# Second mixer's output product: another order of its weight slabs, and two of its pieces in other places among the memory units

## The chip, the cores and the metric

The kernel runs on one core of one Trainium2 chip. The metric is the time of one execution on the device in microseconds. It works on 512 tokens of 1024 features in float32; every large matrix product is made of three products of split numbers (high x high, high x low, low x high), so that a weight slab has to be split in two before TensorE can use it.

## What is computed

The reference chains two blocks of two layers each. The change lies in the second layer of the first block, in the product by `w_out[1]`:

```python
def lru_mixer(h, w_in, conv_w, conv_b, wa, ba, wx, bx, lam):
    p = h @ w_in
    xb, gate, mq = jnp.split(p, [LRU_WIDTH, 2 * LRU_WIDTH], axis=-1)
    xc = centred_depthwise_conv(xb, conv_w, conv_b)
    y = (rg_lru(xc, wa[0], ba[0], wx[0], bx[0], lam[0], False)
         + rg_lru(xc, wa[1], ba[1], wx[1], bx[1], lam[1], True))
    y = y * jax.nn.gelu(gate)
    return y, mq.reshape(B, S, MEM_HEADS, MEM_HEAD_DIM)
...
        mo = memory_attention(mq, mk, mv)
        x = x + jnp.concatenate([mixed, mo], axis=-1) @ w_out[l]
        x = x + squared_relu_mlp(rms_norm(x, mlp_norm[l]), w_up[l], w_down[l])
```

`mixed` has 1024 features (the recurrent part), `mo` 512 (the attention to the memory, 4 heads of 128), so the product has 1536 rows of weights and 1024 outputs.

## The kernel before

Everything is kept transposed: a tile is 128 features by 512 tokens. The program is written engine by engine, with the order of every engine's instructions by hand and semaphores between them; nothing is scheduled by a tool. Each engine goes through its list in order, and an instruction that waits holds up all that stands behind it on that engine.

**Weights.** They come in slabs of 128 x 2048 (16 tiles of 128 x 128). A slab passes through four hands: SP's queue loads it into `w_raw` (line 617), ScalarE rounds it to `w_hi` (`split_high`, line 1260), VectorE takes the rest to `w_lo` (`split_low`, line 1601), TensorE uses both. Each of the three buffers holds two slabs, slab s in place s mod 2. `lo_done` counts the slabs split; `mm_done` counts what TensorE has finished, four to a slab. ScalarE may split slab s when TensorE has finished slab s - 2, and the load of a slab waits until the one two before it has been split.

**The output product of the second mixer** (`out1_1`) has 6 slabs, MIX_O to MIX_O + 5. The 8 output tiles are two halves of 4 blocks, and half h, block b is summed in PSUM bank 4h + b. The 12 tiles of rows are 3 parts of 4: parts 0 and 1 are the recurrent output (`mixL`), part 2 is the memory's (`mixM`). A slab holds one part of one half. The inner function `out(h, part, b)` (matmuls on line 1091) makes one piece: 4 row tiles x 3 split products = 12 matmuls of 128x128 by 128x512. Slab number before: 3h + part. The rest of the text writes a piece as (h, part, b).

**The memory units.** The attention to the memory is 8 units M1[0] to M1[7], of one block of 128 tokens and two heads each. For a unit TensorE does `scores` (L921), `turn_probs` (transposes, L932), `weigh` (L942) and `turn_out` (transposes, L954). Between them VectorE scales and takes maxima (`front`), ScalarE does the exponentials and copies the transposed probabilities (`take_turned`, L1370), VectorE divides (`back`, L1820) and splits the output into `mixM_hi`, `mixM_lo` (`finish`, L1849 and L1851). The units use banks 4 (scores), 5 (turned probabilities) and 6 (outputs). Bank 7 holds a gate of the recurrence until `gate_read` reaches 8.

**TensorE's order before**: (0,0,0..3); the scores of two units; then the 8 units, with (0,1,0), (0,1,1) and (0,1,2) before the weigh of M1[1], M1[2], M1[3]; (0,1,3) behind the last weigh; the last `turn_out`; a wait for its split; (0,2,0..3); then half 1: (1,0), (1,1), (1,2), four blocks each; then the next phase, `up1_1_0` (L843).

**ScalarE and VectorE around it**: slab MIX_O + 2 is split before the units, MIX_O + 3 behind them. Then come the four blocks of half 0: VectorE adds each finished bank to `x` (`add`, L2028, when `mm_done` shows the block of the memory part done), ScalarE writes the scaled `xg_hi` of it (`next_high`, L1462), VectorE `xg_lo` (`next_low`, L2033), and GpSimd sums squares (L648, L652, L654). Behind these four blocks both split slabs MIX_O + 4, MIX_O + 5 and the first of the next phase, then do the four blocks of half 1 in the same way.

## Time and profile before

| | us |
|---|---|
| median of 3 runs without a profile | 3509.99 |
| lowest and highest of them | 3508.42, 3515.12 |
| the profiled execution | 3516.55 |
| its span | 3514.7 |
| TensorE busy in the span | 3331.3 (95%) |
| VectorE busy | 1794.6 (51%) |
| ScalarE busy | 1129.0 (32%) |
| GpSimd busy | 417.9 (12%) |
| mean granted clock of TensorE | 0.957 |

The profile is of one execution of its own, a little longer than the median. Times inside it count from the span's start. A matmul of 128x512 is shown with a length of 0.39 us while the next starts 0.227 us after it, because matmuls overlap in the array; what a row of them costs is read from their starts. The number in brackets at a row's end is how long the engine had been idle before it, and which instruction released it. The granted clock is 1.00 (2.4 GHz) or 0.50 (1.2 GHz), and means lie between.

### The profile page before, as it was taken

How to read it: one execution, taken by the hardware profiler on the slowest of the kernel's cores; microseconds unless marked ns; L12 is line 12 of the kernel's file. 1: busy time of each engine (PE TensorE's matmuls, PEld its weight loads, DVE VectorE, ACT ScalarE, POOL GpSimd, SP SyncE). 2: the span in 40 equal slices, each digit the busy share in tenths (PEclk: the TensorE clock that was granted, in tenths of full speed). 3: DMA queues.
4: the chain of work that ended last, by engine and by line, in shares of the span. 5: the costliest groups of instructions: out<-in, count | busy, mean ns of one | idle time of the engine just before them, and what ended most of it. 6: DMA issues, size and time to landing. Idle time of an engine off the chain costs nothing.

```text
span 3514.7 us, 40951 instructions
## 1 busy us (share of the span) xinstructions
PE 3331.3 (95%) x15310; PEld 2741.9 (78%) x15310; DVE 1794.6 (51%) x1923; ACT 1129.0 (32%) x1292; POOL 417.9 (12%) x391
## 2 busy tenths in 40 slices
PE   7999999999999999999977899999999996699998
PEld 5787888876788878888866688888888885678887
DVE  7764535378552545445355554445434436644444
ACT  3443222267321223223233233223323215223222
POOL 1001000100100060001023410002000202620002
PEclk9999999999999999999986799999999997599999
DMA  3111222322122224222310022224232320012222
GB/s 140 65 51 66 105 99 96 108 96 72 60 96 96 96 96 115 93 106 85 108 60 1 1 96 93 101 82 136 90 108 78 114 96 12 1 55 98 98 92 76
DMA packets 46189, 293.08 MB, mean 83 GB/s; under 512 B 5424, under 2 KB 5936, under 8 KB 17936
## 3 DMA queue, kind: packets, MB, share of 16 engines
q1 hardware_dynamic: 44640, 287.04, 23.2%
q0 software_dynamic: 1456, 4.79, 0.8%
q8 instruction: 61, 1.00, 0.1%
q14 instruction: 32, 0.26, 0.0%
HBM read 289.70 MB, written 2.10 MB: 83 GB/s over the span
## 4 chain that ended last, share of the span: by engine, by line
PE 87%; DVE 6%; POOL 3%; ACT 2%; issue 1%; DVEq 0%; ACTq 0%; POOLq 0%
PE ps L843 72%; POOL dec L754 3%; PE ps L942 2%; PE ps L1027 2%; PE ps L1091 2%; PE ps L1058 1%; PE ps L921 1%; PE ps L1172 1%; PE ps L932 1%; PE ps L890 1%; PE ps L901 1%; DVE mx L1791 0%; DVE w_lo L1601 0%; PE ps L873 0%; ACT sc_n L1359 0%
## 5 line engine op out<-in xcount | busy, mean ns | idle before, releaser
L843 PE MATMUL ps<-xg_hi,w_hi 128*128 128x512 f32 x2304 | 899.8, 391 | 0.0
L843 PE MATMUL ps<-xg_hi,w_lo 128*128 128x512 f32 x2304 | 896.4, 389 | 0.0
L843 PE MATMUL ps<-xg_lo,w_hi 128*128 128x512 f32 x2304 | 896.4, 389 | 0.0
L1601 DVE TENSOR_TENSOR w_lo<-w_raw,w_hi 128x2048 fp32r<-128x2048 f32 (+1 forms) x288 | 671.3, 2331 | 278.0 <-ACT w_hi L1260 278.0
L1260 ACT ACTIVATE w_hi<-w_raw 128x2048 fp32r<-128x2048 f32 (+1 forms) x288 | 545.2, 1893 | 657.5 <-PE ps L843 564.4
L843 PEld LDWEIGHTS ps<-xg_hi,w_hi 128*128 128x128 f32 x2304 | 432.7, 188 | 92.1 <-issue 2.2
L843 PEld LDWEIGHTS ps<-xg_lo,w_hi 128*128 128x128 f32 x2304 | 432.6, 188 | 91.4 <-issue 2.1
L843 PEld LDWEIGHTS ps<-xg_hi,w_lo 128*128 128x128 f32 x2304 | 432.6, 188 | 89.6
L843 PE MATMUL ps<-hid_hi,w_hi 128*128 128x512 f32 x1216 | 473.4, 389 | 0.0
L843 PE MATMUL ps<-hid_hi,w_lo 128*128 128x512 f32 x1216 | 473.0, 389 | 0.0
L843 PE MATMUL ps<-hid_lo,w_hi 128*128 128x512 f32 x1216 | 473.0, 389 | 0.0
L1702 DVE SCALAR_TENSOR_TENSOR x<-ps,x 128x512 f32 (+1 forms) x120 | 83.0, 692 | 403.0 <-PE ps L843 399.8
L1689 DVE TENSOR_TENSOR tmp<-ps,r_bc 128x512 f32<-128x512 f32 x176 | 121.6, 691 | 322.9 <-PE ps L843 307.7
L843 PEld LDWEIGHTS ps<-hid_hi,w_hi 128*128 128x128 f32 x1216 | 228.3, 188 | 48.6 <-issue 1.4
L843 PEld LDWEIGHTS ps<-hid_hi,w_lo 128*128 128x128 f32 x1216 | 228.3, 188 | 47.5
L843 PEld LDWEIGHTS ps<-hid_lo,w_hi 128*128 128x128 f32 x1216 | 228.3, 188 | 46.9
L648 POOL TENSOR_TENSOR ssq<-x 128x512 f32<-128x512 f32 x9 | 9.3, 1038 | 2046.5 <-DVE x L1702 1849.0
L1303 ACT ACTIVATE hid_hi<-tmp 128x512 f32 x88 | 55.7, 632 | 387.6 <-DVE tmp L1692 387.6
L1313 ACT ACTIVATE xg_hi<-x,vec x64 | 46.3, 724 | 350.2 <-DVE x L1702 350.2
L1301 ACT ACTIVATE tmp<-tmp 128x512 f32<-128x512 f32 x88 | 55.6, 632 | 268.9 <-DVE tmp L1689 268.9
L1166 PE MATMUL ps<-fac 64*128 64x128 f32 (+1 forms) x576 | 83.9, 412 | 39.0 <-DVE fac L2120 37.2
L1296 ACT ACTIVATE hid_hi<-tmp 128x512 f32 x64 | 39.6, 633 | 252.9 <-DVE tmp L1676 252.9
(329 smaller groups left out, 3814.6 us busy)
## 6 DMA issues: line engine op xcount, KB each, us to landing
w_raw<-up_dram SPq DMA_DIRECT2D x120, 1024.0 KB, 4.7
w_raw<-in_dram SPq DMA_DIRECT2D x42, 1024.0 KB, 4.8
w_raw<-down_dram SPq DMA_DIRECT2D x32, 1024.0 KB, 4.7
w_raw<-down_dram SPq DMA_DIRECT2D x32, 768.0 KB, 4.2
w_raw<-down_dram SPq DMA_DIRECT2D x32, 640.0 KB, 3.8
w_raw<-out_dram SPq DMA_DIRECT2D x14, 1024.0 KB, 4.7
w_raw<-out_dram SPq DMA_DIRECT2D x8, 768.0 KB, 4.2
w_raw<-memk_dram SPq DMA_DIRECT2D x4, 1024.0 KB, 4.7
```

The lines of the kernel that those rows point to most:

```text
L754: last = pool.tensor_tensor(to[:, :, u, :], (half, mid)[1 - u], (mid, half)[1 - u], ALU.subtract)
L843: last = pe.matmul(ps[:, 2 * q + b, :], (w_hi, w_lo)[wp][:, q, t:t + P], parts[xp], start=(k == 0 and m == 0), stop=(k == p.ktiles - 1 and ...
L942: last = pe.matmul(ps[:, u.o_bank, u.o_col + i * u.d:u.o_col + (i + 1) * u.d], turned(u)[:, kb, i * P:(i + 1) * P], u.v[kb][i], start=(kb ...
L1027: last = pe.matmul(ps[:, bank + b, :], (w_hi, w_lo)[wp][:, j % 2, t:t + P], (xg_hi, xg_lo)[xp][:, k, :], start=(k == 0 and m == 0), stop=( ...
L1091: last = pe.matmul(ps[:, 4 * h + b, :], (w_hi, w_lo)[wp][:, s % 2, t:t + P], parts[xp], start=(part == 0 and k == 0 and m == 0), stop=(par ...
L1166: last = pe.matmul(ps[:, 4 * (j % 2) + hd, c0:c0 + w], keys[:, s0:s0 + P], queries[:, t0:t0 + w], start=True, stop=True)
L1260: act.activation(w_hi[:, q, 0:w], w_raw[:, q, 0:w], ACT.Copy).then_inc(hi_done, 1)
L1301: act.activation(tmp[:, 0, :], tmp[:, 0, :], ACT.Silu).then_inc(silu_done, 1)
L1303: act.activation(pick(hid_hi, j), tmp[:, 1, :], ACT.Copy).then_inc(hid_h, 1)
L1601: dve.tensor_tensor(w_lo[:, q, 0:w], w_raw[:, q, 0:w], w_hi[:, q, 0:w].bitcast(F32), ALU.subtract)\
L1689: dve.tensor_tensor(tmp[:, b, :], ps[:, 2 * q + b, :], r_bc[:], ALU.mult).then_inc(evac, Q // 2)
L1702: dve.scalar_tensor_tensor(out=pick(x, m), in0=ps[:, bank + b, :], scalar=p.alpha, in1=pick(x, m), op0=ALU.mult, op1=ALU.add).then_inc(eva ...
```

## The change

The order of the slabs in memory becomes (0,0), (0,1), (1,0), (0,2), (1,1), (1,2), given by a table `OUT_SLAB`. TensorE's order becomes: (0,0,0..3); in the units (0,1,0) to (0,1,3) before the weighs of M1[1] to M1[4], and (1,0,3) before that of M1[5]; (1,0,0) behind the last weigh; the last `turn_out`; (1,0,1); (1,0,2); (0,2,0..3); (1,1,0..3); (1,2,0..3). New waits stand in front of the pieces of half 1 for their banks: (1,0,3) for `gate_read`, (1,0,0) for `s_read`, (1,0,1) for `pt_ready`, (1,0,2) for `ot_ready`. Every piece, not only the first of a slab, waits for `lo_done`. The number of matmuls is the same. VectorE's adds wait for the slab number of the memory part by the table. The lists of ScalarE, VectorE, GpSimd and SP keep their order.

```diff
+    OUT_SLAB = {(0, 0): 0, (0, 1): 1, (1, 0): 2, (0, 2): 3, (1, 1): 4, (1, 2): 5}
...
             def out(h, part, b):
 
-                s = MIX_O + 3 * h + part
-                if b == 0:
-                    pe.wait_ge(lo_done, s + 1)
-                if h and b == 0 and part == 0:
-                    pe.wait_ge(ot_ready, M1[-1].f + 1)
+                s = MIX_O + OUT_SLAB[h, part]
+                pe.wait_ge(lo_done, s + 1)
...
-                if 1 <= n < 4:
+                if 1 <= n < 5:
                     out(0, 1, n - 1)
+                if n == 5:
+                    pe.wait_ge(gate_read, DT)
+                    out(1, 0, 3)
                 weigh(u)
-            out(0, 1, 3)
+            pe.wait_ge(s_read, M1[-1].n + 1)
+            out(1, 0, 0)
             turn_out(M1[-1])
+            pe.wait_ge(pt_ready, M1[-1].n + 1)
+            out(1, 0, 1)
             pe.wait_ge(ot_ready, M1[-1].f + 1)
+            out(1, 0, 2)
             for b in range(4):
                 out(0, 2, b)
-            for part in range(3):
+            for part in (1, 2):
                 for b in range(4):
                     out(1, part, b)
...
             def add(h, b):
-                dve.wait_ge(mm_done, Q * (MIX_O + 3 * h + 2) + b + 1)
+                dve.wait_ge(mm_done, Q * (MIX_O + OUT_SLAB[h, 2]) + b + 1)
```

The host's layout of `w_out[1]` follows the same table.

On TensorE, in the loop's pass n = 5 before: L932 are the transposes of M1[5]'s probabilities, L921 the scores of M1[7], L954 the transposes of M1[4]'s output, L942 the weighing of M1[5]. The names in brackets are the semaphores waited for.

```order
L932 MATMUL ps<-ident,sc_m 128x128 [waits pt_ready,exp_done]
...
L921 MATMUL ps<-mk_57,proj 128x256 [waits s_read]
...
L954 MATMUL ps<-ident,tmp 128x128 [waits ot_ready,o_ready]
...
L942 MATMUL ps<-mv_59,pt_m 128x128 [waits o_ready,pt_ready]
L942 MATMUL ps<-mv_59,pt_m 128x128 x3
```

The same place in the changed kernel, where the lines have moved by a few (L933, L922, L955, L943; the output product is L1089):

```order
L933 MATMUL ps<-ident,sc_m 128x128 [waits pt_ready,exp_done]
...
L922 MATMUL ps<-mk_57,proj 128x256 [waits s_read]
...
L955 MATMUL ps<-ident,tmp 128x128 [waits ot_ready,o_ready]
...
L1089 MATMUL ps<-mixL_hi,w_hi 128x512 [waits lo_done,gate_read]
L1089 MATMUL ps<-mixL_lo,w_hi 128x512
L1089 MATMUL ps<-mixL_hi,w_lo 128x512
...
L943 MATMUL ps<-mv_59,pt_m 128x128 [waits o_ready,pt_ready]
L943 MATMUL ps<-mv_59,pt_m 128x128 x3
```

Twelve matmuls of the recurrent tiles, piece (1,0,3), now stand between the transposes and the weighing of M1[5].

On TensorE from the last unit's weighing to the next phase, before. `mixL` is the recurrent part's tile, `mixM` the memory's; left out are the other matmuls of the same pieces:

```order
L942 MATMUL ps<-mv_59,pt_m 128x128 [waits o_ready,pt_ready]
...
L1091 MATMUL ps<-mixL_hi,w_hi 128x512
L1091 MATMUL ps<-mixL_lo,w_hi 128x512
L1091 MATMUL ps<-mixL_hi,w_lo 128x512
...
L954 MATMUL ps<-ident,tmp 128x128 [waits ot_ready,o_ready]
...
L1091 MATMUL ps<-mixM_hi,w_hi 128x512 [waits lo_done,ot_ready]
L1091 MATMUL ps<-mixM_lo,w_hi 128x512
L1091 MATMUL ps<-mixM_hi,w_lo 128x512
...
L1091 MATMUL ps<-mixL_hi,w_hi 128x512 [waits ot_ready,lo_done]
...
L1091 MATMUL ps<-mixL_hi,w_hi 128x512 [waits lo_done]
...
L1091 MATMUL ps<-mixM_hi,w_hi 128x512 [waits lo_done]
...
L843 MATMUL ps<-xg_hi,w_hi 128x512 [waits xg_ready,evac,lo_done]
```

And in the changed kernel:

```order
L943 MATMUL ps<-mv_59,pt_m 128x128 [waits o_ready,pt_ready]
...
L1089 MATMUL ps<-mixL_hi,w_hi 128x512 [waits lo_done,s_read]
...
L955 MATMUL ps<-ident,tmp 128x128 [waits ot_ready,o_ready]
...
L1089 MATMUL ps<-mixL_hi,w_hi 128x512 [waits lo_done,pt_ready]
...
L1089 MATMUL ps<-mixL_hi,w_hi 128x512 [waits lo_done,ot_ready]
...
L1089 MATMUL ps<-mixM_hi,w_hi 128x512 [waits lo_done]
L1089 MATMUL ps<-mixM_lo,w_hi 128x512
L1089 MATMUL ps<-mixM_hi,w_lo 128x512
...
L1089 MATMUL ps<-mixL_hi,w_hi 128x512 [waits lo_done]
...
L1089 MATMUL ps<-mixM_hi,w_hi 128x512 [waits lo_done]
...
L844 MATMUL ps<-xg_hi,w_hi 128x512 [waits xg_ready,evac,lo_done]
```

Behind the last unit stood a piece of half 0 and then the memory part; now three pieces of half 1 stand there, two of them between the last transpose and the memory part. Behind the memory part of half 0 stood (1,0), now (1,1).

On ScalarE, from the end of the units, in the changed kernel. L1375 is `take_turned`, L1265 the splitting of a slab (the first is MIX_O + 3, the next three MIX_O + 4, MIX_O + 5 and the next phase's first), L1467 `next_high` of half 0:

```order
L1375 ACTIVATE pt_m<-ps 128x512 [waits o_psum,pt_psum] x2
L1265 ACTIVATE w_hi<-w_raw 128x2048 [waits mm_done,slab_in1]
L1467 ACTIVATE xg_hi<-x,vec 128x512 [waits evac] x4
L1265 ACTIVATE w_hi<-w_raw 128x2048 [waits mm_done,slab_in0]
L1265 ACTIVATE w_hi<-w_raw 128x2048 [waits mm_done,slab_in1]
L1265 ACTIVATE w_hi<-w_raw 128x2048 [waits mm_done,slab_in0]
L1466 ACTIVATE tmp<-x 128x512 [waits evac]
```

These rows stand in the kernel before in the same order, at lines L1370, L1260, L1462 and L1461; what moved is which slab of the product each of them splits.

## Rows read from the trace of the kernel before

**Rows 1.** The page: busy time of each engine; shares of the chain that ended last.

```profile
PE 3331.3 (95%) x15310; PEld 2741.9 (78%) x15310; DVE 1794.6 (51%) x1923; ACT 1129.0 (32%) x1292; POOL 417.9 (12%) x391
...
PE 87%; DVE 6%; POOL 3%; ACT 2%; issue 1%; DVEq 0%; ACTq 0%; POOLq 0%
```

**Rows 2.** Timeline of TensorE, memory units; columns: start us, length, engine, line, tiles, [idle before, releaser].

```profile
886.94 1.05 PE L942 MATMUL ps<-mv,pt_m 128*128 128x128 f32 x8
...
889.46 0.41 PE L954 MATMUL ps<-ident,tmp 128*128 128x128 f32 x2 [0.16 <-DVE mixM_lo L1851]
889.62 0.48 PE L1091 MATMUL ps<-mixL_hi,w_hi 128*128 128x512 f32 x1
...
892.46 1.05 PE L942 MATMUL ps<-mv,pt_m 128*128 128x128 f32 x8
...
895.23 1.06 PE L942 MATMUL ps<-mv,pt_m 128*128 128x128 f32 x8
...
898.11 0.41 PE L954 MATMUL ps<-ident,tmp 128*128 128x128 f32 x2 [0.53 <-DVE mixM_lo L1851]
898.36 1.06 PE L942 MATMUL ps<-mv,pt_m 128*128 128x128 f32 x8
...
900.95 0.41 PE L954 MATMUL ps<-ident,tmp 128*128 128x128 f32 x2 [1.09 <-DVE mixM_lo L1851]
...
903.90 0.41 PE L954 MATMUL ps<-ident,tmp 128*128 128x128 f32 x2 [1.03 <-DVE mixM_lo L1851]
904.14 1.06 PE L942 MATMUL ps<-mv,pt_m 128*128 128x128 f32 x8
904.96 0.48 PE L1091 MATMUL ps<-mixL_hi,w_hi 128*128 128x512 f32 x1
...
907.80 0.38 PE L954 MATMUL ps<-ident,tmp 128*128 128x128 f32 x2
909.15 0.50 PE L1091 MATMUL ps<-mixM_hi,w_hi 128*128 128x512 f32 x1 [0.98 <-DVE mixM_lo L1851]
```

**Rows 3.** Timeline of TensorE, half 1's product and the next phase's first matmul.

```profile
920.21 0.39 PE L1091 MATMUL ps<-mixL_hi,w_hi 128*128 128x512 f32 x1
...
952.85 0.39 PE L843 MATMUL ps<-xg_hi,w_hi 128*128 128x512 f32 x1
```

**Rows 4.** Timeline of VectorE in the same stretch.

```profile
908.67 0.42 DVE L1851 TENSOR_TENSOR mixM_lo<-ps,mixM_hi 128x256 fp32r<-128x256 f32 x1
910.00 2.29 DVE L1601 TENSOR_TENSOR w_lo<-w_raw,w_hi 128x2048 fp32r<-128x2048 f32 x1 [0.90 <-ACT w_hi L1260]
...
920.47 0.69 DVE L2028 TENSOR_TENSOR x<-ps,x 128x512 f32<-128x512 f32 x1 [1.27 <-PE ps L1091]
...
923.77 3.00 DVE L1601 TENSOR_TENSOR w_lo<-w_raw,w_hi 128x2048 fp32r<-128x2048 f32 x1 [0.30 <-ACT w_hi L1260]
```

**Rows 5.** Timeline of ScalarE in the same stretch.

```profile
921.20 0.73 ACT L1462 ACTIVATE xg_hi<-x,vec 128x512 fp32r<-128x512 f32 x1 [2.00 <-DVE x L2028]
921.83 1.90 ACT L1260 ACTIVATE w_hi<-w_raw 128x2048 fp32r<-128x2048 f32 x1
```

**Rows 6.** Timeline of GpSimd in the same stretch.

```profile
923.00 1.62 POOL L654 TENSOR_TENSOR ssq<-ssq,sq 128x512 f32<-128x512 f32 x1
```

**Rows 7.** Timeline of VectorE at 310 us.

```profile
309.60 2.29 DVE L1601 TENSOR_TENSOR w_lo<-w_raw,w_hi 128x2048 fp32r<-128x2048 f32 x1 [1.05 <-ACT w_hi L1260]
```

**Rows 8.** Timeline of TensorE behind the idle times at 852 and 312 us.

```profile
852.39 0.80 PE L1091 MATMUL ps<-mixL_hi,w_hi 128*128 128x512 f32 x1 [3.30 <-DVE proj L1951]
...
858.03 0.39 PE L1091 MATMUL ps<-mixL_lo,w_hi 128*128 128x512 f32 x1
...
312.03 0.79 PE L843 MATMUL ps<-mixA_hi,w_hi 128*128 128x512 f32 x1 [3.31 <-DVE w_lo L1601]
...
315.43 0.40 PE L843 MATMUL ps<-mixA_hi,w_lo 128*128 128x512 f32 x1
```

**Rows 9.** Busy time in a stretch: us, engines, granted clock (PEclk), DMA.

```profile
852.40:857.70 5.30, 5.30 (x13) 4.15 (x14) 4.06 (x4) 3.54 (x4) 0.00 (x0) 0.50 0.13 36
```

More of the change, by code:

```diff
@@ L2376, in layout @@
             rows = [f["w_out"][1][512 * k:512 * (k + 1)] for k in range(3)]
-            a["out1_1"] = np.concatenate([slabs_of(r, range(4 * h, 4 * h + 4), 4, 4) for h in range(2) for r in rows])
+            a["out1_1"] = np.concatenate([slabs_of(rows[k], range(4 * h, 4 * h + 4), 4, 4)
+                                          for h, k in ((0, 0), (0, 1), (1, 0), (0, 2), (1, 1), (1, 2))])
         for h in range(2):
```

## The prediction

> **What bounds the kernel now.** I read the page first: the span is 3514.7 us, TensorE is busy in 95% of it and makes 87% of the chain that ended last [rows 1]. The change touches one stage, the second mixer's output product, so I looked for it in the timeline of TensorE: it runs from the memory units (886 us) to the first matmul of the next phase at 952.85. Inside the units the reader should see small matmuls, each unit closed by its "weigh" (L942), and in front of it a transpose (L954) that in the later units waits about 1 us for VectorE [rows 2]. From 909.15 the output product runs as one stream. From 920.21, where the second half's product begins, to 952.85, where L843 takes over, lie 144 matmuls in 32.64 us, 0.227 us each, with no idle time [rows 3]. So TensorE itself is the bound here: a wait that is added to it, or removed, moves everything behind it by its length, as long as nothing else is late. Last I read what TensorE could wait for, the splits of the weight slabs on ScalarE (w_hi) and VectorE (w_lo).
>
> I call the pieces by half, part and block: (1,0,3) is half 1, part 0, block 3, which is 12 matmuls. Warm and in line a piece takes 12 x 0.227 = 2.72 us.
>
> **Part 1, two pieces move into the units.** Piece (0,1,3) goes from behind the loop into the fifth unit, and (1,0,3) into the sixth. The unit with a piece that lies between the weighs at 886.94 and 892.46 takes 5.52 us. The two units without one, 892.46 to 895.23 and 895.23 to 898.36, take 2.77 and 3.13 [rows 2]. The two grow by 2.75 + 2.39 = 5.14 us, for work that costs 2 x 2.72 = 5.44 in the stream: a gain of 0.30 us. It comes mostly from the wait of 0.53 us at 898.11, which a piece covers (at 889.46 with a piece it is 0.16). The units at 900.95 and 903.90 keep their waits of 1.09 and 1.03 us: nothing is put in front of those transposes.
>
> The new waits of (1,0,3) are for its bank, which the recurrence's gates had read before the units began, and for slab 2, whose w_lo was made before the first unit. I cost both at nothing. The further semaphore waits, one for each piece, are for slabs already split; nothing too.
>
> **Part 2, the end of the units.** Before, from the last weigh at 904.14 come (0,1,3) at 904.96, the last transpose at 907.80, a wait of 0.98, and the memory part of half 0 at 909.15: 5.01 us from the weigh to the next product [rows 2]. Now (1,0,0) stands in the place of (0,1,3), and behind the transpose comes (1,0,1), which needs nothing of the last unit's output. It starts as a piece did at 889.62, 0.16 behind its transpose at 889.46, so the stretch is 904.96 - 904.14 + 2.84 + 0.16 = 3.82 us (2.84 is 892.46 less 889.62). Gain 1.19 us. The product at 909.15 also needed 11.06 us for its 48 matmuls instead of 10.88, which (0,2) in mid-stream will not; the piece (1,0,1) pays 0.12 of that. Gain of part 2: 1.25 us, and with part 1 **1.55 us**.
>
> Does its cover hold? (1,0,2) waits until VectorE has taken the last unit. Before, its last operation on it began at 908.67, 0.87 after the transpose at 907.80, and took 0.42 [rows 4]: 1.29 us, against 3.00 us of (1,0,1) and the hand-over. The memory part (0,2) now reads slab 3. Its w_lo stands behind that last operation on VectorE and takes 2.29 us (at 910.00, where it had to wait 0.90 for w_hi; ScalarE now gets its release earlier, since slab 1 is used up in the fifth unit). It is done 1.29 + 2.29 = 3.6 us after the transpose, and needed after two pieces, 5.7 us. Margin 2.1 us, no wait.
>
> **Part 3, what is late next: slab 4.** Only TensorE's program and the order of the slabs in memory change. ScalarE and VectorE still split slab 3, then do the four blocks of half 0's sum and norm, and only then split slab 4. Before, TensorE left half 0 at 920.21 and went on with slab 3, split long before; slab 4 had 10.9 us more. Now slab 3 is the memory part of half 0 itself, and behind it comes (1,1), which needs slab 4 at once. The transfer, SP's queue and the buffers do not delay it, since slab 2 is used up 10.9 us earlier. The chain that does is in the rows, counted from 920.21: VectorE's last add of half 0 begins at 920.47; ScalarE's last xg_hi of that half begins at 921.20 and its w_hi of slab 4 at 921.83, for 1.90 [rows 5]; VectorE's w_lo of slab 4 begins at 923.77 and takes 3.00 us, so it ends at 926.77 [rows 4]. Each of these follows from TensorE's end of half 0 by fixed steps, and they stay as they are. TensorE starts 0.14 after such an end: elsewhere a w_lo from 309.60 for 2.29 us [rows 7] released a product at 312.03 [rows 8]. The new stall is 926.77 + 0.14 - 920.21 = **6.70 us**. Where could it be shorter? The 3.00 us stand beside a GpSimd addition of 1.62 us at 923.00 [rows 6]; without that overlap w_lo takes 2.29, and the stall 5.99. But the GpSimd steps hang on the same adds, so I keep 3.00.
>
> The row shows 3.00 against 2.29 us. The Trainium skill ("GPSIMD Engine Reference", Specifications) says that GpSimd shares its access to SBUF with VectorE, and that an instruction of VectorE with two SBUF inputs can suffer; this one has two. By that page the 3.00 stays, and the stall is 6.70; taken as chance it would be 5.99.
>
> Behind it, slab 5 has everything early. Slab 6, the next phase's first, waits for TensorE's end of (1,1), as it did before. The last half's adds, the norm and the next phase follow at their old distances, and there was no idle time between 920.21 and 952.85 that could swallow the stall.
>
> **Part 4, the clock behind the stall.** The two comparable idle times are in the trace. After 3.30 us of idle the product at 852.39 ran 13 starts in 5.64 us (to 858.03) instead of 2.95; granted clock from 852.4 to 857.7: 0.50, the lower of the two levels, 1.2 GHz [rows 9]. Cost 2.69 us. After 3.31 us the product at 312.03 ran 8 starts in 3.40 us (to 315.43) instead of 1.81: cost 1.59 us [rows 8]. A wait of 0.98 us (909.15) cost nothing of this kind [rows 2]. No row shows a stall of 6.7 us before a dense product; it is longer than both, so the clock falls. I take the mean, **2.15 us**; for the range I go 0.4 and 0.3 us beyond the two, to 1.2 and 3.0, because two rows are few.
>
> The Trainium skill ("TensorE: Matmul & The Clock Gate", Part 1: The HAM clock gate) says that one kernel showed 6, 11 or 14 slow matmuls from run to run. At 0.20 us more for each, that would make the term 1.2, 2.2 or 2.8 us instead of the 2.15 of the rows. Its section Why this matters for your kernels asks for no long idle gaps between bursts of matmuls: a rule against this change, and the rows agree with 1.59 and 2.69 us after 3.3 us of idle.
>
> **Sum.** 6.70 + 2.15 - 1.55 = +7.3 us. The profiled execution had a span of 3514.7 and took 3516.55; the median of the runs without a profile is 3509.99. The step is in TensorE's stream in both, so I add it to the median: 3509.99 + 7.3 = **3517.3 us**, 0.21% slower. All ends: 5.99 + 1.2 - 2.0 = +5.2 to 6.70 + 3.0 - 1.3 = +8.4, with the gain taken at 1.3 to 2.0.
>
> **Rivals.** *A, the same stall, cheaper.* w_lo runs in 2.29 and the slow matmuls are as few as at 312.03: 5.99 + 1.59 - 1.55 = +6.0, 3516.0, which is within 0.2%. Against it: the GpSimd row of 1.62 us hangs on the same chain.
>
> *B, no stall, and the intended gain alone.* This is the case on the other side. It holds if slab 4's split does not stand behind half 0's sum in fact: then TensorE runs through and only the closed waits remain, -1.55 us, 3508.4. The point that decides is whether w_lo of slab 4 ends before TensorE finishes (0,2). ScalarE runs its program in order, and w_hi of slab 4 stands there behind four xg_hi that need the finished blocks. Everything in rows 4 and 5 speaks against B. To be faster by 0.2% one would need -7.0 us, more than all idle time of this stage.
>
> *C, the stall and a second wait.* Slab 3 late too, or the last unit's output late for (1,0,2), because the units' pattern shifts: each us beyond the margin of 2.1 adds itself. With 2 us over it: +9.3, 3519.3. For it: VectorE's order puts w_lo of slab 3 behind the last unit. Against: the margin.
>
> **How the numbers follow.** Forecast 0.72, A 0.13, C 0.10, B 0.05. The bound of 0.2% (about what a measurement of this kernel can tell from no change) is 7.0 us, and my sum lies on its edge. Of the forecast's 0.72 a little more than half is above it; C is all above, A and B are all within. Slower 0.52, same 0.45, faster 0.03. The range takes in the ends +5.2 and +8.4, one us and a half on either side since the three runs before span 3508.42 to 3515.12, and most of C: 3513.5 to 3520.
>
> **What would show it.** Right: in TensorE's timeline one wait of some 6.5 us for w_lo in front of the product of half 1, part 1, then 6 to 14 matmuls at 0.43 us; the wait of 0.98 behind the last transpose gone; the two waits near 1 us still there; the next phase's first matmul 7 us later than 952.85. Wrong: that wait under 5 us, which would mean that ScalarE or VectorE reach slab 4 another way than through half 0's norm; or waits for slab 3; or a clock that stays at 1.00 behind the stall.

## The result and the profile after

| | before | changed |
|---|---|---|
| median, us | 3512.08 (17 runs) | 3520.89 (17 runs) |
| lowest and highest | 3502.27, 3517.31 | 3517.98, 3524.81 |
| span of the profiled execution | 3514.7 | 3522.4 |
| TensorE busy in it | 3331.3 | 3333.7 |
| mean granted clock in it | 0.957 | 0.957 |

The ratio is 1.0028, with a 95% interval of 1.002 to 1.0036: 7 to 13 us slower. The forecast had the direction and the mechanism, but it said 3517.3 us with 3513.5 to 3520.0 around it, and the measured 3520.89 lies outside.

The page of the changed kernel, the same lines as in [rows 1]:

```profile
PE 3333.7 (95%) x15310; PEld 2743.0 (78%) x15310; DVE 1794.6 (51%) x1923; ACT 1129.2 (32%) x1292; POOL 418.2 (12%) x391
...
PE 87%; DVE 6%; POOL 3%; ACT 2%; issue 1%; DVEq 0%; ACTq 0%; POOLq 0%
```

Nothing shows at this level: the change is 0.3% of the span. The view that shows it is the list of what TensorE waited for. It has one line that the kernel before has not (us in total, times, longest), and lacks that of 0.98 us in front of the product:

```profile
PE ps L1089 <- DVE w_lo L1606: 6.4, 1, 6.4
```

The timeline of TensorE in the changed kernel, the stretch of [rows 2] and [rows 3] (L955 is the transpose of a unit's output, L943 the weighing, L1089 the output product, L844 the next phase):

```profile
896.41 1.05 PE L943 MATMUL ps<-mv,pt_m 128*128 128x128 f32 x8
...
898.93 0.41 PE L955 MATMUL ps<-ident,tmp 128*128 128x128 f32 x2 [0.16 <-DVE mixM_lo L1856]
899.09 0.48 PE L1089 MATMUL ps<-mixL_hi,w_hi 128*128 128x512 f32 x1
901.93 1.05 PE L943 MATMUL ps<-mv,pt_m 128*128 128x128 f32 x8
...
904.81 0.41 PE L955 MATMUL ps<-ident,tmp 128*128 128x128 f32 x2 [0.52 <-DVE mixM_lo L1856]
904.97 0.48 PE L1089 MATMUL ps<-mixL_hi,w_hi 128*128 128x512 f32 x1
907.81 1.05 PE L943 MATMUL ps<-mv,pt_m 128*128 128x128 f32 x8
...
913.10 0.41 PE L955 MATMUL ps<-ident,tmp 128*128 128x128 f32 x2 [1.03 <-DVE mixM_lo L1856]
913.34 1.06 PE L943 MATMUL ps<-mv,pt_m 128*128 128x128 f32 x8
914.15 0.48 PE L1089 MATMUL ps<-mixL_hi,w_hi 128*128 128x512 f32 x1
916.99 0.38 PE L955 MATMUL ps<-ident,tmp 128*128 128x128 f32 x2
917.13 0.48 PE L1089 MATMUL ps<-mixL_hi,w_hi 128*128 128x512 f32 x1
...
933.36 0.39 PE L1089 MATMUL ps<-mixM_hi,w_lo 128*128 128x512 f32 x1
940.15 0.80 PE L1089 MATMUL ps<-mixL_hi,w_hi 128*128 128x512 f32 x1 [6.41 <-DVE w_lo L1606]
...
943.72 0.39 PE L1089 MATMUL ps<-mixL_hi,w_lo 128*128 128x512 f32 x1
...
963.69 0.39 PE L844 MATMUL ps<-xg_hi,w_hi 128*128 128x512 f32 x1
```

Read it from the bottom. Half 0's last matmul starts at 933.36, the next one is due 0.23 later, at 933.59, and comes at 940.15: a stall of 6.56 us. Then 8 starts take 3.57 us (to 943.72) instead of 1.81: slow matmuls for 1.76 us. Further up, the wait in front of 917.13 is gone (in [rows 2] it was 0.98 at 909.15), while the transposes still wait.

To compare kernels I use one length, the **stage**: from the transpose in front of the fifth unit's weighing (894.98 before, 898.93 here) to the next phase's first matmul (952.85, 963.69). It is 57.87 us before and 64.76 here, **+6.89 us**. What stands ahead of 894.98 is the same work in both kernels and took 3.95 us more in this execution; TensorE is busy 4.81 us longer with the same matmuls up to there (853.58 against 848.77), so more of them were slow.

Where the stall comes from, on VectorE, ScalarE and GpSimd, as in [rows 4], [rows 5] and [rows 6]:

```profile
933.85 0.69 DVE L2033 TENSOR_TENSOR x<-ps,x 128x512 f32<-128x512 f32 x1 [1.27 <-PE ps L1089]
934.46 2.36 DVE L2038 SCALAR_TENSOR_TENSOR xg_lo<-x,vec,xg_hi 128x512 fp32r<-128x512 f32 x2
937.13 5.16 DVE L1606 TENSOR_TENSOR w_lo<-w_raw,w_hi 128x2048 fp32r<-128x2048 f32 x2 [0.31 <-ACT w_hi L1265]
```

```profile
934.58 0.72 ACT L1467 ACTIVATE xg_hi<-x,vec 128x512 fp32r<-128x512 f32 x1 [1.99 <-DVE x L2033]
935.21 3.70 ACT L1265 ACTIVATE w_hi<-w_raw 128x2048 fp32r<-128x2048 f32 x2
```

```profile
936.35 1.60 POOL L655 TENSOR_TENSOR ssq<-ssq,sq 128x512 f32<-128x512 f32 x1
```

The distances from TensorE's end of half 0 (933.59) are those that the rows of before gave from 920.21, to 0.02 us: last add 0.26, last xg_hi 0.99, w_hi of slab 4 1.62, its w_lo 3.54. Both slabs, 4 and 5, are now split in one go (5.16 us for two), since slab 5 waits for nothing either.

### The profile page after: what moved, and what is told of

The parts are those of the page before. It is cut to its first block, busy times and chain, and to the rows that moved or that the text cites. A ratio compares the mean times of both kernels' runs of the same rounds, so it can differ in the third digit from the quotient of the medians.

```text
span 3522.4 us, 40953 instructions
## 1 busy us (share of the span) xinstructions
PE 3333.7 (95%) x15310; PEld 2743.0 (78%) x15310; DVE 1794.6 (51%) x1923; ACT 1129.2 (32%) x1292; POOL 418.2 (12%) x391
## 4 chain that ended last, share of the span: by engine, by line
PE 87%; DVE 6%; POOL 3%; ACT 2%; issue 1%; DVEq 0%; ACTq 0%; POOLq 0%
PE ps L844 72%; POOL dec L755 3%; PE ps L943 2%; PE ps L1028 2%; PE ps L1089 2%; PE ps L1059 1%; PE ps L922 1%; PE ps L1177 1%; PE ps L933 1%; PE ps L891 1%; PE ps L902 1%; DVE w_lo L1606 1%; DVE mx L1796 0%; PE ps L874 0%; PE ps L955 0%
## 5 line engine op out<-in xcount | busy, mean ns | idle before, releaser
L844 PE MATMUL ps<-xg_hi,w_hi 128*128 128x512 f32 x2304 | 899.6, 390 | 0.0
L844 PE MATMUL ps<-xg_hi,w_lo 128*128 128x512 f32 x2304 | 896.4, 389 | 0.0
L844 PE MATMUL ps<-xg_lo,w_hi 128*128 128x512 f32 x2304 | 896.4, 389 | 0.0
L1265 ACT ACTIVATE w_hi<-w_raw 128x2048 fp32r<-128x2048 f32 (+1 forms) x288 | 545.0, 1893 | 649.6 <-PE ps L844 564.4
L844 PEld LDWEIGHTS ps<-xg_hi,w_hi 128*128 128x128 f32 x2304 | 432.6, 188 | 91.7 <-issue 2.2
L844 PEld LDWEIGHTS ps<-xg_lo,w_hi 128*128 128x128 f32 x2304 | 432.5, 188 | 91.7 <-issue 1.9
L844 PEld LDWEIGHTS ps<-xg_hi,w_lo 128*128 128x128 f32 x2304 | 432.5, 188 | 89.8
L844 PE MATMUL ps<-hid_hi,w_hi 128*128 128x512 f32 x1216 | 473.3, 389 | 0.0
L844 PE MATMUL ps<-hid_hi,w_lo 128*128 128x512 f32 x1216 | 473.1, 389 | 0.0
L844 PE MATMUL ps<-hid_lo,w_hi 128*128 128x512 f32 x1216 | 473.0, 389 | 0.0
L844 PEld LDWEIGHTS ps<-hid_hi,w_hi 128*128 128x128 f32 x1216 | 228.2, 188 | 48.6 <-issue 1.4
L844 PEld LDWEIGHTS ps<-hid_hi,w_lo 128*128 128x128 f32 x1216 | 228.3, 188 | 47.5
L844 PEld LDWEIGHTS ps<-hid_lo,w_hi 128*128 128x128 f32 x1216 | 228.3, 188 | 47.2
```

The costliest lines, as they stand in the source:

```text
L844: last = pe.matmul(ps[:, 2 * q + b, :], (w_hi, w_lo)[wp][:, q, t:t + P], parts[xp], start=(k == 0 and m == 0), stop=(k == p.ktiles - 1 and ...
L1265: act.activation(w_hi[:, q, 0:w], w_raw[:, q, 0:w], ACT.Copy).then_inc(hi_done, 1)
```

## Experiments

Five questions. Is the stall the place of slab 4's split, and nothing else? Does the reordering cost or gain by itself? What does the clock take? Does GpSimd lengthen the stall? And why is the median further off than the stage? The table is worked out from TensorE's timelines: the stage as defined above, the stall within it (the start behind it, less the start that was due), and the rest of the program, from the next phase's first matmul to the last matmul.

| kernel | stage | stall | slow matmuls' cost | rest of the program | median, us (before beside it) |
|---|---|---|---|---|---|
| before | 57.87 | none | 0 | 2553.57 | 3512.08 |
| before, again | 57.84 | none | 0 | 2547.09 | one time only |
| changed | 64.76 | 6.56 | 1.76 | 2550.28 | 3520.89 (3512.08) |
| changed, again | 64.78 | 6.57 | 1.77 | 2550.18 | 3521.59 (3511.20) |
| slab 4 split early | 56.44 | none | 0 | 2545.07 | 3505.74 (3511.26) |
| stall in the old order | 67.41 | 6.56 | 2.98 | 2547.64 | 3518.99 (3511.26) |
| stall filled | 63.19 | filled | 0 | 2545.04 | 3513.67 (3511.26) |
| split before the last block | 61.54 | 3.44 | 1.66 | 2550.13 | 3515.85 (3511.26) |
| GpSimd later | 64.48 | 5.89 | 2.15 | 2547.19 | one time only |
| both splits moved | 56.44 | none | 0 | 2545.06 | 3502.86 (3511.20) |

The slow matmuls' cost is the stage less 57.87, less the stall, plus 1.43 in the kernels with the new order, which is what that order gains by the first experiment. It is what is left over, so I priced it a second time from the starts behind each stall, less 0.227 us for each: 1.76, 1.73, 3.01, 1.66 and 2.06 for the five rows with a stall from the top. The two ways agree within 0.1 us.

### Slab 4's split ahead of half 0's sum

On ScalarE, and in the same way on VectorE (with `add` and `next_low`):

```diff
             split(MIX_O + 3)
+            split(MIX_O + 4)
             for b in range(4):
                 next_high(0, b)
-            split(MIX_O + 4)
```

> The changed kernel, with the split of slab MIX_O + 4 (ScalarE's w_hi and VectorE's w_lo) moved ahead of the four blocks of half 0's sum and norm. Theory S (the loss is the wait of 6.56 us for that slab's w_lo and the slow clock behind it): the wait of TensorE in front of piece (1,1,0) is gone, its clock stays at 1.00 there, and the time goes from 8.8 us above the kernel before to 1.2 us below it (-0.5 to -2, same as before within the measurement). Rival R (the order itself costs: a semaphore wait on each piece, half 1's banks filled beside the units): the wait goes, and the kernel stays 2 us or more above the kernel before. Rival C (the clock in later stages got worse because everything moved by some 8 us): stays above as well, and the trace shows the stage itself no longer than before.

The wait is gone and the stage takes 56.44 us: 8.32 less than the changed kernel, 1.43 less than the kernel before. TensorE goes from the memory part to (1,1,0) without a break:

```profile
928.40 0.39 PE L1089 MATMUL ps<-mixM_hi,w_lo 128*128 128x512 f32 x1
928.63 0.39 PE L1089 MATMUL ps<-mixL_hi,w_hi 128*128 128x512 f32 x1
```

VectorE pays 2.29 us for it where it had time:

```profile
919.95 2.29 DVE L1606 TENSOR_TENSOR w_lo<-w_raw,w_hi 128x2048 fp32r<-128x2048 f32 x1 [4.42 <-ACT w_hi L1265]
922.16 0.68 DVE L2033 TENSOR_TENSOR x<-ps,x 128x512 f32<-128x512 f32 x1
923.46 0.69 DVE L2033 TENSOR_TENSOR x<-ps,x 128x512 f32<-128x512 f32 x1 [0.61 <-PE ps L1089]
```

The first add of half 0 comes late, and the second one waits for TensorE again. The median is 3505.74 against 3511.26, ratio 0.9989 (0.998 to 0.9998): faster than the kernel before, by 5.5 us of the medians, where S had 0.5 to 2. The interval runs from 0.7 to 7 us and holds the stage's 1.43. The rivals R and C, which had it above the kernel before, fall. The loss in the stage hangs on where one split stands in two engines' lists; the new order of TensorE alone is worth 1.43 us there.

### The stall in the old order

```diff
-            split(MIX_O + 3)
             for b in range(4):
                 next_high(0, b)
+            split(MIX_O + 3)
             split(MIX_O + 4)
```

> The kernel before, with the split of slab MIX_O + 3 moved behind the four blocks of half 0's sum and norm on ScalarE and VectorE; TensorE's order is untouched. It puts the same late slab into the old order. Theory S: TensorE waits 6.5 us in front of piece (1,0,0) and then runs 6 to 14 matmuls slowly (1.5 to 2.7 us); since nothing is gained in the units, the kernel is slower than before by 8 to 9.3 us, which is 1.2 us more than the stall and the clock cost in the changed kernel. Rival R: it is slower by clearly less than the changed kernel (under 7 us), because a part of that loss comes with the new order.

```profile
921.70 0.39 PE L1091 MATMUL ps<-mixM_hi,w_lo 128*128 128x512 f32 x1
928.49 0.80 PE L1091 MATMUL ps<-mixL_hi,w_hi 128*128 128x512 f32 x1 [6.40 <-DVE w_lo L1601]
```

The same stall, 6.56 us, appears in front of (1,0,0). This time 14 matmuls ran slowly and cost 2.98 us, so the stage is 9.54 us longer than before (67.41 less 57.87), a little over the 8 to 9.3 expected. The ratio is 1.0022 (1.0012 to 1.0031), a median 7.7 us higher. R asked for clearly less than the changed kernel, under 7. The stage speaks against it; the median alone, with an interval from 4 to 11 us, does not decide.

### The stall filled with matmuls

```diff
+            pe.wait_ge(evac, half_out(0, 0))
+            for _ in range(28):
+                pe.matmul(ps[:, 0, :], mixM_hi[:, 0, 0:P], mixL_hi[:, 0, :], start=True, stop=True)
             for part in (1, 2):
```

> The changed kernel, with 28 further matmuls (128x128 by 128x512, 0.227 us each, 6.3 us together, result into bank 0 and never used) in front of piece (1,1,0), after the first sum of half 0 has been taken. They lie in the wait for slab 4, so the wait stays as long, but TensorE is busy in it. Theory S with a clock term of 1.5 to 2.7 us: piece (1,1,0) starts as late after half 0's end as in the changed kernel (6.6 us), the clock stays at 1.00, and the time is 1.5 to 2.7 us below the changed kernel, so 5.5 to 7 above the kernel before. Rival (the clock costs nothing, the wait is all): no gain over the changed kernel.

Timeline of TensorE, and the stretch's granted clock (columns: us, busy us of PE, PEld, DVE, ACT, POOL, PEclk, DMA share, GB/s):

```profile
933.84 6.51 PE L1127 MATMUL ps<-mixL_hi,mixM_hi 128*128 128x512 f32 x28
940.46 0.50 PE L1089 MATMUL ps<-mixL_hi,w_hi 128*128 128x512 f32 x1
```

```profile
933.80:940.50 6.70, 6.59 (x30) 5.11 (x28) 6.10 (x5) 4.34 (x3) 4.18 (x3) 1.00 0.00 0
```

Piece (1,1,0) starts 6.62 us after it was due, as late as in the changed kernel, but the clock stays at 1.00 and the stage is 1.57 us shorter, at the low end of what was expected. The clock behind the stall is a cost of its own; doing useless work in the wait takes it away. The median, though, lies 7.2 us below the changed kernel's (6.4 when each is taken against the kernel before beside it), not 1.5 to 2.7, and only 2.4 above the kernel before (ratio 1.0005, 0.9996 to 1.0014), not 5.5 to 7. The stage cannot account for that. The column on the rest of the program can: 2545.04 instead of 2550.28. I come back to it below.

### The split one block earlier

```diff
-            for b in range(4):
+            for b in range(3):
                 next_high(0, b)
             split(MIX_O + 4)
+            next_high(0, 3)
```

> The changed kernel, with the split of slab MIX_O + 4 moved ahead of the last of the four blocks of half 0's sum and norm only (behind three). Theory S: the chain to w_lo hangs on the end of block 2 instead of block 3, 2.72 us earlier; with the GpSimd overlap the wait in front of (1,1,0) becomes 3.2 to 3.9 us instead of 6.56, still with slow matmuls behind it (1.5 to 2.7 us). Time 2.7 to 3.4 us below the changed kernel. Rival (the wait is set by something other than the place of the split, for instance the slab's transfer): the wait stays at 6 us or more.

```profile
931.84 0.80 PE L1089 MATMUL ps<-mixL_hi,w_hi 128*128 128x512 f32 x1 [3.28 <-DVE w_lo L1607]
```

One block earlier takes 3.12 us off the stall (6.56 to 3.44), of which 2.72 are the block and 0.4 a w_lo that overlaps less with GpSimd. About as many matmuls are slow as behind the stall of twice the length: the clock term does not grow with the wait. The stage is 3.22 us shorter than the changed kernel's, and the median is 4.6 above the kernel before (ratio 1.0014, 1.0005 to 1.0023), against 3.67 by the stage. It is 4 to 5 us below the changed kernel's, where 2.7 to 3.4 were expected.

### GpSimd out of the way

```diff
                 n = gained(MIX_NEXT)
+                pool.wait_ge(lo_done, MIX_O + 5)
                 squares(n, lambda m: pool.wait_ge(evac, 3 * m + half_out(0, 0)), 4)
```

> The changed kernel, with GpSimd's sums of squares of half 0 held back until slab MIX_O + 4 is split, so that GpSimd does nothing beside VectorE in the wait. If the overlap is what lengthens VectorE's operations: w_lo of that slab takes 2.29 us instead of 2.9 to 3.0, the two xg_lo before it 1.3 instead of 2.36, and TensorE's wait in front of (1,1,0) is 5.9 us instead of 6.56. Rival (these are slow for another reason, such as the transfer that runs then): they keep their length, and the wait stays at 6.5 us.

```profile
929.45 1.62 DVE L2039 SCALAR_TENSOR_TENSOR xg_lo<-x,vec,xg_hi 128x512 fp32r<-128x512 f32 x2
932.12 4.49 DVE L1607 TENSOR_TENSOR w_lo<-w_raw,w_hi 128x2048 fp32r<-128x2048 f32 x2 [1.05 <-ACT w_hi L1266]
```

```profile
934.50 3.02 POOL L649 TENSOR_TENSOR ssq<-x 128x512 f32<-128x512 f32 x1 [219.84 <-DVE w_lo L1607]
937.70 1.04 POOL L653 TENSOR_TENSOR sq<-x 128x512 f32 x1 [0.18 <-POOL ssq L649]
```

The two w_lo take 4.49 us instead of 5.16, and the stall is 5.89 us instead of 6.56: the overlap is worth 0.67 us, and the step of the prediction that kept 3.00 rather than 2.29 us was right. The two xg_lo went from 2.36 to 1.62 us (1.3 was expected), but VectorE waited for w_hi behind them all the same. GpSimd's own multiplication, begun while VectorE's second w_lo ran, took 3.02 us; the next one, alone, took 1.04. The w_lo that was running was not lengthened. In the one execution there is, the stage gains only 0.28, because 9 matmuls were slow instead of 8.

### Both splits out of the way

The first experiment's kernel, with one more step on VectorE:

```diff
-            split(MIX_O + 2)
             front(M1[0], 0)
             front(M1[1], 1)
+            split(MIX_O + 2)
```

> The kernel of the run with slab MIX_O + 4 split early, and besides, on VectorE, the w_lo of slab MIX_O + 2 moved behind the score fronts of the first two memory units, where TensorE had waited 4.12 us for the first of them. Theory S (a split that VectorE has queued ahead of what TensorE waits for sets these waits): the wait of 4.12 us in front of the second unit's scores falls under 1.5 us, TensorE's clock stays at 1.00 there more often, and the kernel is 3 to 5 us faster than the one with slab MIX_O + 4 early, so 4.5 to 7 us faster than the kernel before (0.13 to 0.2%). Rival (the wait is set by ScalarE or by the exponentials behind): the wait moves to the next transposes and the time stays.

In the kernel before TensorE waited 4.12 us for the first unit's scores to be read, at 871.13, since VectorE had the w_lo of slab 2 queued ahead of that:

```profile
871.13 1.69 PE L921 MATMUL ps<-mk,proj 128*128 128x256 f32 x4 [4.12 <-DVE sc_m L1788]
...
868.19 2.29 DVE L1601 TENSOR_TENSOR w_lo<-w_raw,w_hi 128x2048 fp32r<-128x2048 f32 x1 [4.10 <-ACT w_hi L1260]
870.40 0.68 DVE L1788 TENSOR_SCALAR sc_m<-ps 128x512 f32<-128x512 f32 x1
```

Now:

```profile
868.26 1.13 PE L922 MATMUL ps<-mk,proj 128*128 128x256 f32 x4 [0.79 <-DVE sc_m L1793]
870.31 0.66 PE L933 MATMUL ps<-ident,sc_m 128*128 128x128 f32 x4 [0.92 <-ACT sc_m L1364]
...
872.71 1.16 PE L943 MATMUL ps<-mv,pt_m 128*128 128x128 f32 x8 [0.87 <-ACT pt_m L1375]
```

The wait falls to 0.79, and about 0.9 us of it comes back as two waits of 0.92 and 0.87 (they were 0.36 and 0.57). The granted clock from 862 to 876 is 1.00 in this kernel and 0.88 in the kernel before. The median is 3502.86 against 3511.20, ratio 0.9972 (0.9961 to 0.9984): the fastest of all kernels here, 8 us under the kernel before and 18 under the changed one. Against the kernel of the first experiment that is 2.8 to 2.9 us, a little under the 3 to 5 expected; against the kernel before it is more than the 4.5 to 7 expected, because the first experiment's median was lower than expected too.

### Why the median moved by more than the stage

> The changed kernel again, unchanged, beside the others. Question: is its distance to the kernel before the 6.9 us by which its output product stage is longer (6.56 us wait + 1.8 slow matmuls - 1.4 gained), or is there something besides, since the first comparison gave 8.8? Theory S, all in the stage: over the two sets of runs together 6.5 to 8.5 us, with one to three us either way from how many matmuls run slowly in stages that the change does not touch. Rival (a later stage is hurt as well): 9 us or more again, and a later stage that is longer in this profile than in that of every kernel without the stall.

The stage repeats to 0.02 us (64.78), the rest of the program to 0.1 (2550.18). The median does too: 3521.59 against 3511.20, ratio 1.0032 (1.002 to 1.0044), 10.4 us. That is more than S's 6.5 to 8.5, so S misses here; but R's later stage that is longer than in every kernel without the stall is not there either, since the one profile of the kernel before had 2553.57. The next runs look at that length.

> The kernel before, once more with a profile. In the profiles so far the stretch from the end of this stage to the program's end took 2550.2 us in the changed kernel (2550.3 in its first profile), 2545.06 in the three kernels in which this stage had no slow matmuls, and 2553.6 in the one profile of the kernel before. Theory P (from this stage on, how many matmuls run slowly at later waits depends on where those waits fall against the moments at which the clock changes): the kernel before has several such lengths, and this profile shows another one than 2553.6, between 2545 and 2551; its output product stage is 57.87 us again. Rival: 2553.6 again, a property of the kernel.

The same program has a rest of 2547.09 us in this profile and of 2553.57 in the first one, with the same stage. The difference of 6.5 us is not spread out. It is 0.45 us at 1852 us and 3.3 at 1886, in the neighbourhood attention of the second block's first layer, where TensorE waits often; most of what is left arises between 2910 and 3080, in that block's second layer. Here is one stretch of each execution, the first profile and then the second, in which 53 of the 54 matmuls are the same (columns as above):

```profile
1848.00:1862.00 14.00, 11.19 (x54) 9.28 (x53) 7.06 (x8) 4.62 (x12) 3.97 (x2) 0.62 0.00 1
```

```profile
1847.50:1861.50 14.00, 8.11 (x54) 6.79 (x54) 8.69 (x9) 4.62 (x12) 5.06 (x2) 0.74 0.00 1
```

The clock is 0.62 in one and 0.74 in the other, and TensorE is busy for 11.19 and 8.11 us with them. So theory P's condition holds: the kernel before has more than one length. The rival, 2553.57 as a property of the kernel, falls.

Over the whole of the rest the same shows: in the first profile of the kernel before and in that of the first experiment TensorE is busy for 2428.01 and 2416.04 us with the same 10986 matmuls (the view counts the one at its edge in the second):

```profile
952.85:3506.40 2553.55, 2428.01 (x10986) 2004.67 (x10985) 1220.32 (x1187) 747.64 (x756) 355.83 (x343) 0.95 0.24 81
```

```profile
950.39:3495.50 2545.11, 2416.04 (x10987) 1995.35 (x10985) 1220.62 (x1187) 747.47 (x756) 355.97 (x343) 0.96 0.24 82
```

Then pure delays, in the kernel before, 5, 10 and 15 matmuls between the halves:

```diff
+            pe.wait_ge(evac, half_out(0, 0))
+            for _ in range(5):
+                pe.matmul(ps[:, 0, :], mixM_hi[:, 0, 0:P], mixL_hi[:, 0, :], start=True, stop=True)
             for part in range(3):
```

> The kernel before, with 5 further matmuls (128x128 by 128x512, result into bank 0 and never used) between the two halves of the output product. They are in line, so the stage is 5 x 0.227 = 1.1 us longer and nothing else is touched. Theory P: the stretch behind the stage takes one of several lengths between 2545 and 2554 us in its profile, and the median differs from the kernel before by anything from -3 to +5 us. Rival (a pure delay adds its own length): +1.1 us.

> The same with 10 further matmuls: the stage is 2.3 us longer. Theory P: the stretch behind the stage is not the same as with 5 or 15 more, and the median differs from the kernel before by something other than 2.3 us, from -2 to +7. Rival (a pure delay adds its own length): +2.3 us, with the later stretch as in the others.

> The same with 15 further matmuls: the stage is 3.4 us longer. Theory P: since the clock's changes come at steps of their own, this one should resemble the kernel before more than those with 5 and 10 do, in the length behind the stage. Rival: +3.4 us, later stretch as in the others.

| further matmuls | stage | rest of the program | median (before 3513.17) | ratio |
|---|---|---|---|---|
| 5 | 58.98 | 2549.31 | 3513.31 | 1.0001 (0.9991 to 1.001) |
| 10 | 60.11 | 2551.33 | 3515.40 | 1.0005 (0.9995 to 1.0015) |
| 15 | 61.22 | 2550.48 | 3515.31 | 1.0013 (1.0002 to 1.0023) |

The stages grew by 1.11, 2.24 and 3.35 us, as 5, 10 and 15 times 0.227 ask for. The rest was another length each time, within 2549.3 to 2551.3, so the rivals' "later stretch as in the others" falls. The medians went up by 0.1, 2.2 and 2.1 us, the ratios by 0.4, 1.8 and 4.6 us; the intervals are 7 us wide and hold the pure delay in all three. That 15 would resemble the kernel before more than 5 and 10 was not borne out. So these medians show no more than the delay itself, and could not have shown 2 or 3 us more. What the profiles show is that the rest of the program varies by up to 8.5 us (2545.04 to 2553.57), with the same matmuls in it.

In these profiles the rest goes with what happened in this stage: 2545.04 to 2545.07 in all three kernels whose slab 4 did not keep TensorE idle under the new order, 2550.13 to 2550.28 in the three with 7 to 8 slow matmuls behind a stall, 2547.19 and 2547.64 in the two with 9 and 14, although within a group what came ahead of the stage differed by up to 7 us. This fits medians that are further apart than the stages: split early against changed, 15.2 us by the medians (14.3 when each is taken against the kernel before beside it), of which 8.3 are the stage and 5.2 the rest in their profiles. That TensorE's idle time and the slow matmuls in one stage set where later waits fall against the clock's changes is argued from these lengths, not shown, and the kernel before speaks against it as the whole cause: with the same stage twice it has rests 6.5 us apart, and the old order without a stall has five rests in five profiles, 2547.09 to 2553.57. For the changed kernel against the kernel before it leaves 8.8 and 10.4 us of the medians against 6.9 of the stage; the 2 to 3.5 us between them stay open, since the kernel before has no single length to compare with. Nor is the difference one shift of all executions: in the first comparison the highest of the two kernels lie 7.5 us apart, near the stage's 6.9, and the lowest 15.7.

There is a second source of spread that the experiments did not look for, ahead of the stage. In the profiles the stage begins between 889.08 us (15 further matmuls) and 899.16 (stall filled) in kernels that are the same up to there. One wait near the start differs most; here it is in the kernel before and in the first experiment's, with what VectorE and GpSimd did ahead of it:

```profile
40.16 1.94 PE L997 MATMUL ps<-ident,proj 128*128 128x128 f32 x8 [6.25 <-DVE proj L1657]
28.16 4.70 DVE L1894 SCALAR_TENSOR_TENSOR rope_r<-rope_k,rope_r 128x512 f32<-128x512 f32 x2
28.50 3.81 POOL L631 TENSOR_TENSOR mem_sq<-mem_raw 128x2048 f32<-128x2048 f32 x1 [27.66 <-PE ps L790]
```

```profile
35.25 1.07 PE L998 MATMUL ps<-ident,proj 128*128 128x128 f32 x8 [0.16 <-DVE proj L1662]
28.23 1.42 DVE L1899 SCALAR_TENSOR_TENSOR rope_r<-rope_k,rope_r 128x512 f32<-128x512 f32 x2
29.69 3.88 POOL L632 TENSOR_TENSOR mem_sq<-mem_raw 128x2048 f32<-128x2048 f32 x1 [28.85 <-PE ps L791]
```

Where GpSimd's multiplication begins before VectorE is through, VectorE's next operation stands for most of its length. Over the 13 profiles TensorE's wait is 6.05 to 6.39 us in seven, 3.27 to 3.71 in five and 0.16 in one; in the changed kernel it was 6.15 once and 3.65 once. So the spread is not the clock's alone. How much of this wait reaches the end is not shown: the profile with 0.16 came to the stage only 1.04 us before the kernel before (893.94 and 894.98).

## Why the prediction was right or wrong, point by point

**What bounds the kernel.** Right. TensorE's stream carried the stall one to one: stages differ by the stall, the slow matmuls and the closed waits, and by nothing else (with the slow matmuls priced from their starts, the sums close to 0.1 us in every kernel with a stall).

**Part 1, pieces into the units: +0.30 us forecast, about 0.2 measured, for other reasons.** From the weighing at 896.41 to that at 907.81 are 11.40 us; before, 5.90 from 892.46 to 898.36 [rows 2]. Less 5.44 for the two pieces this is a loss of 0.06. The transpose behind the new piece still waited 0.52 us, where I had read 0.16 from 889.46, so the piece did not cover that wait: VectorE's division began 1.52 us after the fifth unit's weighing instead of 1.16. That belongs to the fifth unit and not to the piece, for it was so in the kernel before (896.75 behind the weighing at 895.23), as it is now (903.45 behind 901.93). Its cause stays open. The last two units took 5.53 us (907.81 to 913.34) instead of 5.78, which gave 0.25 back. The fifth unit's division in the kernel before:

```profile
896.75 0.43 DVE L1820 TENSOR_TENSOR tmp<-ps,rec 128x256 f32<-128x256 f32 x1 [0.21 <-DVE rec L1817]
```

**Part 2, the end of the units: 1.25 forecast, 1.26 measured.** 3.79 us from the weighing at 913.34 to the product at 917.13, against 3.82 worked out and 5.01 before. The cover held: w_lo of slab 3 was done before it was needed, and no wait for it stands in the timeline. Together with part 1 the gain is 1.43 us against 1.55.

**Part 3, the stall: 6.70 forecast, 6.56 measured.** The chain was read from rows of a kernel that did not have the stall, and each step stood at the same distance within 0.02 us. What is missing of the 6.70 is the hand-over: from the start of w_lo to TensorE are 3.02 us (937.13 to 940.15), where I had added 3.00 and 0.14. Rival A's 5.99 was met only where GpSimd was held back (5.89), and B and C did not occur.

**Part 4, the clock: 2.15 forecast, 1.76 measured** in the changed kernel, 1.66 to 2.98 over the five profiles with a stall. The two rows from before, 1.59 and 2.69, bounded it but for the 2.98, though the stall was twice as long as theirs. I had written that no row shows a longer stall before a dense product, but the trace of the kernel before has one, the program's own start:

```profile
14.78 0.77 PE L1027 MATMUL ps<-xg_hi,w_hi 128*128 128x512 f32 x1 [14.78 <-DVE w_lo L1601]
...
18.30 0.40 PE L1027 MATMUL ps<-xg_hi,w_lo 128*128 128x512 f32 x1
```

8 starts in 3.52 us instead of 1.81: cost 1.71 after 14.78 us of idle. It speaks against a term that grows with the stall. Where I noted that the Trainium skill ("TensorE: Matmul & The Clock Gate", Part 1: The HAM clock gate) gives 6, 11 or 14 slow matmuls for one kernel, the runs here agree: 7 to 14 behind the stalls, and 8 to 14 at the start of the program, which is the same in all kernels here.

**The sum: +7.3 forecast, +6.9 in the stage.** So far every term was within its bounds.

**The step that failed is the last one, from the stage to the time and its range.** I added the sum to 3509.99, the median of three runs, and allowed one and a half us on either side, "since the three runs before span 3508.42 to 3515.12". The same kernel before has medians of 3512.08, 3511.26, 3511.20 and 3513.17 in the four comparisons, and single runs from 3502.27 to 3518.16. Two of its profiles differ by 6.5 us in stages that the change does not touch. What stands ahead of the stage differs by up to 10 us, and I had put both at nothing. Of the 3.6 us by which I missed, 2.1 are the base's median, and 1.5 the larger difference (8.8 by the medians for a sum of 7.3), whose cause stays open. The terms' bounds described the stage; the range had to describe a median of the whole program, with the clock's share of every other waiting stage in it. 3513 to 3524 would have been honest. With the chances it is the same: I gave "within 0.2%" 0.45 because my sum lay on that edge, while the interval measured starts at 1.002. And the 0.03 for faster had no case behind it, since I had put both A and B within 0.2%.

## What to carry to other kernels

When work is reordered on one engine, follow each input of the new neighbour back through the other engines' lists: here the product was moved ahead, its slab's split was not, and it stood behind four steps that waited for the product itself. Moving one split on each of two engines turned a loss of 9 us into a gain of about 5 (0.7 to 7 by its interval), and the same question asked of another wait gave a further 3. A stall costs its length and then a few slow matmuls, about as many for a wait of 3.4 us as for one of 6.6, and the range of a prediction must hold the spread of the whole program's median, not of the stage alone.

## What the runs showed of the hardware

The rest of the program, without any change in it, took 2545.04 to 2553.57 us, and in the same kernel 2547.09 and 2553.57. TensorE was busy for 2416.04 to 2428.01 us with the same matmuls in it, and where two profiles part, its mean granted clock is 0.62 in one and 0.74 in the other. I had taken that as noise of one or two us.

GpSimd and VectorE delay each other, and in these rows it is the one that begins second that is lengthened, by a little less than the time for which the first still runs. VectorE's subtraction of 128x2048 took 2.29 us alone and 3.00 when GpSimd's addition had 0.85 left (923.77 to 924.62); GpSimd's multiplication of 128x512 took 1.04 us alone and 3.02 when VectorE's subtraction had 2.11 left (934.50 to 936.61), and that subtraction kept its length. The Trainium skill ("GPSIMD Engine Reference", Specifications) names this contention for instructions with two SBUF inputs; the traces agree.
